# Where the three units of seven products stand in a gate pair: 3, 4 and 5 instead of 3, 5 and 6

## What is computed

```python
# first block: four branches, each with its own gate of 2048 columns
xn = rms_norm(x, norm_mix_g)
proj = xn @ w_in                                   # the last 4 * 2048 columns are gate_logits
gates = sigmoid(gate_logits.reshape(b, s, 4, d))
merged = sum(gates * branches, axis=2)
x = x + merged @ w_out
...
# second block
h2 = rms_norm(x, norm2_g)
x = x + (silu(h2 @ w_gate) * (h2 @ w_up)) @ w_down  # 5632 hidden columns
```

## Time and profile before

| | |
|---|---|
| median of three runs | 2453.77 us |
| the profiled execution, its own time | 2455.18 us |
| its span in the profile | 2453.4 us |
| TensorE busy | 2434.3 us (99%), 11614 matmuls |
| VectorE busy | 1896.9 us (77%) |
| ScalarE busy | 1264.9 us (52%) |
| granted TensorE clock, mean | 0.999 |

### The profile page before, as it was taken

The page is one execution under the profiler, slowest core; times in us unless marked ns, Lnnn a source line. Parts: engine busy times, 40 slices in busy tenths (PEclk is TensorE's granted clock), DMA queues, the critical chain, the costliest instruction groups (busy, mean ns, idle before and its releaser), DMA issues.

```text
span 2453.4 us, 28949 instructions
## 1 busy us (share of the span) xinstructions
PE 2434.3 (99%) x11614; PEld 2027.6 (83%) x11614; DVE 1896.9 (77%) x1798; ACT 1264.9 (52%) x1309; POOL 65.7 (3%) x67
## 2 busy tenths in 40 slices
PE   9999999999999999999999999999999999999999
PEld 8888878888888888888888888788878878888787
DVE  5775588888756795886875558876898989888897
ACT  5545545545444543544543458784555545545553
POOL 0410000000000000000000000000200000000000
PEclk9999999999999999999999999999999999999999
DMA  8555556666655565665665555444555665566654
GB/s 253 172 188 172 165 186 198 193 201 200 233 185 188 195 201 189 205 193 188 202 197 189 204 184 187 155 147 162 177 186 201 195 202 189 193 202 194 197 193 155
DMA packets 233908, 467.19 MB, mean 190 GB/s; under 512 B 14192, under 2 KB 25984, under 8 KB 233390
## 3 DMA queue, kind: packets, MB, share of 16 engines
q1 hardware_dynamic: 232222, 460.09, 57.6%
q10 hardware_dynamic: 1552, 5.25, 0.6%
HBM read 463.20 MB, written 2.10 MB: 190 GB/s over the span
## 4 chain that ended last, share of the span: by engine, by line
PE 92%; DVE 3%; issue 2%; ACT 1%; POOL 0%; DMA 0%; POOLq 0%; SPq 0%; DVEq 0%; ACTq 0%
PE acc L465 10%; PE acc L474 10%; PE acc L1749 10%; PE acc L467 10%; PE acc L1753 10%; PE acc L1750 10%; PE acc L494 5%; PE acc L500 2%; PE tp L494 2%; PE sd L494 2%; PE acc L1809 2%; PE acc L1805 2%; PE acc L1806 2%; PE sd L1806 1%; PE sd L1809 1%
## 5 line engine op out<-in xcount | busy, mean ns | idle before, releaser
L450 DVE TENSOR_TENSOR wlo<-raw,whi 128x2048 fp32r<-128x2048 f32 (+1 forms) x361 | 812.7, 2261 | 164.6 <-ACT whi L441 162.8
L441 ACT ACTIVATE whi<-raw 128x2048 fp32r<-128x2048 f32 (+1 forms) x361 | 674.3, 1884 | 184.9 <-PE acc L1753 71.9
L465 PE MATMUL acc<-whi,opA_hi 128*128 128x512 f32 x768 | 304.8, 397 | 0.0
L467 PE MATMUL acc<-whi,opA_lo 128*128 128x512 f32 x768 | 299.4, 390 | 0.0
L1749 PE MATMUL acc<-whi,opA_hi 128*128 128x512 f32 x744 | 291.0, 391 | 3.6 <-ACT silu_gate L1498 1.8
L1750 PE MATMUL acc<-whi,opA_lo 128*128 128x512 f32 x744 | 290.1, 390 | 0.0
L1753 PE MATMUL acc<-wlo,opA_hi 128*128 128x512 f32 x744 | 203.0, 391 | 2.0 <-DVE wlo L450 2.0
L474 PE MATMUL acc<-wlo,opA_hi 128*128 128x512 f32 x768 | 192.6, 392 | 0.2 <-DVE wlo L450 0.2
L1749 PE MATMUL acc<-whi,opB 128*128 128x512 f32 x448 | 176.2, 393 | 4.8 <-ACT silu_gate L1498 4.8
L2284 DVE TENSOR_TENSOR t_low<-t_sum,t_hi 128x2048 fp32r<-128x2048 f32 x79 | 180.4, 2284 | 0.1
L1750 PE MATMUL acc<-whi,opB 128*128 128x512 f32 x448 | 174.5, 389 | 0.0
(11 more groups left out here) (431 smaller groups left out, 4075.8 us busy)
## 6 DMA issues: line engine op xcount, KB each, us to landing
raw<-in_w_in SPq DMA_DIRECT2D x66, 1024.0 KB, 5.4
raw<-in_w_mlp_up SPq DMA_DIRECT2D x64, 1024.0 KB, 5.2
raw<-in_w_mlp_down SPq DMA_DIRECT2D x64, 1024.0 KB, 5.0
raw<-in_w_in SPq DMA_DIRECT2D x120, 512.0 KB, 4.7
raw<-in_w_gate SPq DMA_DIRECT2D x88, 512.0 KB, 3.8
raw<-in_w_up SPq DMA_DIRECT2D x88, 512.0 KB, 4.7
raw<-in_w_down SPq DMA_DIRECT2D x88, 512.0 KB, 4.6
raw<-in_w_out SPq DMA_DIRECT2D x32, 1024.0 KB, 5.0
```

Source lines behind the costliest of these rows:

```text
L441: eng.activation(whi[:, u % SPL, k, 0:cols], raw[:, u % RAW, k, 0:cols], ACT.Copy).then_inc(hi_split, share(k))
L450: eng.tensor_tensor(wlo[:, u % RAW, k, 0:cols], raw[:, u % RAW, k, 0:cols], whi[:, u % SPL, k, 0:cols].bitcast(F32), ALU.subtract).then_in ...
L465: eng.matmul(acc[:, pair, m, 0:cols], hi[:, kt + i, m * P:(m + 1) * P], whi[:, s, i, 0:cols], start=first and i == 0, stop=False)
L467: eng.matmul(acc[:, pair, m, 0:cols], lo[:, kt + i, m * P:(m + 1) * P], whi[:, s, i, 0:cols], start=False, stop=False)
```

## The change

Three tuples. In gate pairs the three units of seven products are v3, v4 and v5 instead of v3, v5 and v6, for the second block (`GATE_SEVEN`) and the first (`BRANCH_SEVEN`). The first gate pair of the second block, for which activation sums aren't ready in time for all places, had the last two of the tuple, v5 and v6; it now has only the last, v5.

```diff
-GATE_SEVEN, DOWN_SEVEN = (3, 5, 6), (3, 5)
+GATE_SEVEN, DOWN_SEVEN = (3, 4, 5), (3, 5)
 FIRST_SEVEN, QUARTERS = (2, 4, 5), 3
-BRANCH_SEVEN, LATER = (3, 5, 6), 3
+BRANCH_SEVEN, LATER = (3, 4, 5), 3
...
-                PAIRS.append(Pair(len(PAIRS), "gate", unit, PAIR_UNITS, GATE_SEVEN if PAIRS else GATE_SEVEN[1:], 0,
+                PAIRS.append(Pair(len(PAIRS), "gate", unit, PAIR_UNITS, GATE_SEVEN if PAIRS else GATE_SEVEN[2:], 0,
```

## The result

The changed kernel takes 2439.18 us (2438.27 to 2440.44, four runs) against 2453.8 us (2453.24 to 2454.59, four runs) for the kernel before: 0.9941 of its time, with an interval from 0.9923 to 0.9958. Predicted were 2438.7 us and a range from 2436.5 to 2445. The profiled execution took 2439.19 us, its span 2437.5 us, where the kernel before had 2455.18 and 2453.4.

What follows compares the result with a forecast made beforehand. TensorE was taken as the bound, through its matmul count and its waits at gate pair borders. -11.9 - 3.2 - 0.7 + 0.7 = -15.1 us took the profiled 2455.18 to 2440.1, the median to 2438.7; range 2436.5 to 2445.

Steps and rivals of the forecast that it cites:

- What bounds the kernel: TensorE, busy for 2434.3 of 2453.4 us: only the number of matmuls and TensorE's waits can move the time.
- The two lines of the earlier trace: TensorE's waits at gate pair borders: 6.6 us in 11 for the silu, 1.8 us in 3 for the sigmoid.
- Edit 1: Last unit of seven products at v5 instead of v6 in all 17 gate pairs: -11.9, -3.2 and -0.7 us.
- The margin of the silu: At a gate pair's border, TensorE could start on bank (0,1) at 2062.56, wanted at 2063.50: margin 0.94 us.
- Edit 2: Units of seven products in a row, v3, v4, v5: no cost, margin 0.1 us in three pairs before down pairs.
- this as a sign: In the profile after, v5's first sum on VectorE starts right at the end of v3, released by TensorE.
- Edit 3: First gate pair of the second block has one unit of seven products instead of two: three more matmuls, +0.7 us.
- The sum: All terms together, -15.1 us: the profiled execution goes from 2455.18 to 2440.1 us.
- Rival C: v5's sums wait for v3's buffer, low split 3.2 us late in 16 pairs: 2490 us; chance 0.06, shared with similar causes.
- Rival B: At the pair's border, bank (0,1) stays as late as now, the wait only moves: 2453.8 us; chance 0.06.

Runs made afterwards that it cites:

- row_at_6: Changed kernel with the three units of seven products at v4, v5, v6 in both blocks (first pair of the second: v6 alone): 1.0002 of the kernel before.
- apart_ends_5: Changed kernel with v2, v4 and v5 as units of seven products in the first block's six gate pairs: 0.9938 of the kernel before.
- pad_v2: Changed kernel with two useless adds of 1024 elements per partition on VectorE at v2 of eight gate pairs: 2446.95 us, 0.9969 of the kernel before.
- one_buffer: Changed kernel with weight sums waiting for the end of the last unit of seven products, not the second last, outside scaled pairs: 2590.26 us.
- after_again: The changed kernel, unchanged, timed once more: median 2438.7 us, 0.9938 of the kernel before.
- corr_first: Kernel before, with VectorE's correction of bank (0,1) put ahead of the split of the next pair's first unit: 2450.3 us, 0.9986.
- first_two: Changed kernel with v4 and v5 in the second block's first gate pair, its sum buffers swapped in that block: 2440.03 us.
- sums_later: Changed kernel with the first block's last activation sums moved behind the split of its first gate pair's v0: median 2437.35 us, 0.9933 of the kernel before.

## Why the prediction was right, point by point

**What bounds the kernel** was read rightly. The two lines of the earlier trace rows carried the whole gain: each half of the change took its own away with the time expected.

**Edit 1, the end of the last unit of seven products.** Put at 11 x 1.08, 3 x 1.08 and 3 x 0.22. In the profile after, v0 behind a gate pair takes 5.44 to 5.45 us in all 14 places, against 6.49 to 6.55: 1.04 to 1.11 each. The step that took over, the correction of bank (0,0) by the end of its own bank, was put at 3.84 us ahead of the new pair and came 3.87 ahead. The margin of the silu was put at 0.94 and is 1.0. `row_at_6` and, for the first block, `apart_ends_5` show that the place of the last unit does it, and not the row. At the branch products TensorE's timeline has

```profile
410.16 0.62 PE L1753 MATMUL acc<-wlo,opA_hi 128*128 128x512 f32 x2
410.62 0.39 PE L465 MATMUL acc<-whi,opB 128*128 128x512 f32 x1
410.84 0.39 PE L467 MATMUL acc<-whi,opB 128*128 128x512 f32 x1
```

with 0.46 and 0.22 us between them, for the earlier trace rows with 0.56 and 0.34: the 0.22 is won there as well.

**Edit 2, the row of three.** Put at no cost, with 0.1 us to spare in three pairs. Counted from the start of v0 (2052.61), v3's sums started at 10.30 (predicted 10.31), v4's at 16.88 (16.9), v5's at 23.46 (23.5); the low split of v5 was over at 27.93 (27.9), wanted at 28.10 (28.09). v5 took 4.76, 4.78 and 4.80 us in the three pairs, so 0.06 us were lost. That the margin was really this thin, and at this place, is what `pad_v2` shows. That the forecast of no cost held so exactly is thus in part luck: a tenth or two of a microsecond more on VectorE would have been seen in these three pairs.

The release of the buffer was read rightly too, and the changed kernel shows it. In a pair that isn't the last of its part VectorE reaches v5's sums early and stands idle (VectorE's timeline; "issue" says that the profile names no releaser):

```profile
2032.47 1.22 DVE L2267 TENSOR_TENSOR t_sum<-raw 128x1024 f32<-128x1024 f32 x1 [1.10 <-issue]
```

TensorE's v3 of that pair ends, and v4 starts, at 2032.21. There are ten such idle times in front of v5's sums, 9.8 us together, and in all ten the sums start 0.26 us after v3's end; in the kernel before there is none. The prediction named this as a sign. It put these sums at v3's end itself and their margin at 1.5 us, which is 1.4. And `one_buffer`, where each buffer is waited for one such unit longer, costs its 3.26 us at the place named.

The rule by which edit 2 would have cost some 200 us, that of the drain from the Trainium skill, "VectorE: DVE Perf Modes", section "The DRAIN you can't avoid", does not describe this kernel: it takes 2439.2 us and not 2650, and a unit's five operations in a row again take 6.58 us from start to start (2062.91 to 2069.49). The prediction left out the last sentence of the paragraph that it drew on, by which a next operation that is not held starts earlier.

**Edit 3.** Put at +0.7. From the start of that pair's v0 to the start of the next pair's v0 it is 43.58 us before and 44.26 after: +0.68.

**The sum.** Put at -15.1 for the profiled execution, whose span fell by 15.9. Of this 15.1 lie between the first gate pair and the end. The other 0.83 are there before any changed unit: v0 of the first gate pair starts at 323.72 instead of 324.55. The change has no part in them. All but 0.04 of them are there by the program's second matmul on weights, which starts at 7.60 instead of 8.39, behind the load of x and its transposes; over all profiles of this case that matmul starts between 7.60 and 9.04, and in `after_again`, the same program, at 8.04. The median of the runs is 14.6 lower, and 0.5 above the forecast, well inside its own scatter of 2.2.

**Where sizes were off**, it was in the experiments: `corr_first` won 0.25 per pair instead of 0.33, `first_two` lost 1.50 in v5 instead of 0.9, and `one_buffer` took 49 us more than expected. Rival C's time was too low for the same two reasons: what a wait costs beyond its idle time, 0.3 us here, and the clock. The prediction priced neither; neither bears on the forecast, since the waits of 0.60 us had their full cost of 1.08 read from a row.

**Rival B**, that the wait only moves, is refuted for the changed kernel by its list of waits. It is a real way to fail, though: `corr_first` and `sums_later` both end in it, the one for three quarters of what it set out to win and the other for a quarter.

## What to carry to other kernels

When a short wait returns once per tile, follow its releaser back until you come to an event whose time is set by the place of a piece of work and not by its length. Moving that piece earlier shifts the whole queue behind it, up to the next thing that it waits for (here 1.9 us of the 5.44, which was enough). Reordering a queue that is late as a whole mostly changes the name of what is waited for (here it won 0.25 of 1.08 us). Before work is packed closer on the helper engine, add up its lead at each step from start-to-start times in the timeline, for the tile with the most extra work: here this gave the margins to within 0.1 us, which is enough to tell a free change from one that costs 2.6 us per tile.

## What the runs showed of the hardware that was not expected

**A wait can cost more than itself, through the clock.** In `one_buffer` 21 of the 32 waits of 3.26 us on TensorE came with a stretch at the lower clock level, and 11 with none: in the pair shown above, the first of two equal waits was followed by 21 matmuls at the usual pace and the second by matmuls 0.43 apart. The cost was about 1.6 us for each stretch of 3.4 us. Behind the shorter waits of this case, the 14 of 0.6 us before the change and the six of up to 1.49 us in `pad_v2`, the profiles show no such stretch.

**The same program falls or doesn't.** The one wait of 2.0 us in the first gate pair stands in the profile of the kernel before, where the matmuls some 2.8 us after it start 0.42 us apart (TensorE's timeline):

```profile
327.62 0.73 PE L1753 MATMUL acc<-wlo,opA_hi 128*128 128x512 f32 x2 [2.01 <-DVE wlo L450]
...
330.39 0.63 PE L1750 MATMUL acc<-whi,opA_lo 128*128 128x512 f32 x1
330.81 0.63 PE L1749 MATMUL acc<-whi,opA_hi 128*128 128x512 f32 x1
```

and in that of `after_again`, where they don't:

```profile
327.72 0.73 PE L1753 MATMUL acc<-wlo,opA_hi 128*128 128x512 f32 x2 [2.00 <-DVE wlo L450]
...
330.14 0.39 PE L1749 MATMUL acc<-whi,opA_hi 128*128 128x512 f32 x1
330.36 0.39 PE L1750 MATMUL acc<-whi,opA_lo 128*128 128x512 f32 x1
```

That unit took 9.37 or 9.38 us in three of the profiles (the kernel before, the changed kernel, `first_two`) and 7.75 to 7.80 us in eight others with the same wait, `after_again` among them, which is the changed kernel's own program. So 1.6 us of the difference of two spans of this kernel can be the clock alone, about a tenth of what the change brings. The comparison above is not touched by it: both profiles, before and after, have the fall. What decides whether the clock falls after a wait of 2.0 us is open.
